# Wide matmuls over both activation halves, one pair (MLP: two panels) sooner in a two-block transformer kernel

## What is computed

```python
def swiglu(h, w_gate, w_up, w_down):
    return (jax.nn.silu(h @ w_gate) * (h @ w_up)) @ w_down
# block 1, per layer (D_FF = 2816), twice, with rmsnorm in front
x = x + 0.5 * swiglu(rmsnorm(x, norm_ffn1[layer]), ffn1_gate[layer], ffn1_up[layer], ffn1_down[layer])
# block 2 (D_FF_2 = 4096)
v2 = rmsnorm_2(h, g_pre_mlp[i])
f = jnp.square(jax.nn.relu(v2 @ w_up[i])) @ w_down[i]
```

## Time and profile before

| what | value |
| --- | --- |
| median of 3 runs | 1740.2 us (1740.07 to 1741.12) |
| the profiled execution: its time | 1740.54 us |
| its span in the trace | 1738.7 us |
| TensorE busy | 1711.1 us, 98% of the span |
| VectorE busy | 1129.2 us, 65% |
| ScalarE busy | 963.3 us, 55% |
| GpSimd busy | 139.7 us, 8% |
| HBM traffic | 166 GB/s over the span |
| granted TensorE clock, mean | 0.998 of full |

### The profile page before, as it was taken

One profiled execution on the slowest core, in us unless ns is written; L12 is line 12 of the kernel. 1 busy time (PEld: TensorE's weight loads), 2 busy tenths in 40 slices (PEclk: granted clock), 3 DMA queues, 4 the chain that ended last, 5 costly groups with the idle time before them and its releaser, 6 DMA issues.

```text
span 1738.7 us, 29426 instructions
## 1 busy us (share of the span) xinstructions
PE 1711.1 (98%) x12582; PEld 1537.9 (88%) x12582; DVE 1129.2 (65%) x1315; ACT 963.3 (55%) x1127; POOL 139.7 (8%) x124
## 2 busy tenths in 40 slices
PE   9999999999999999999999999999999999999996
PEld 8888999898889888999898889987898889988896
DVE  6666789575567556689675556664455566775657
ACT  5544696564446444587564446644445564654445
POOL 1000004000000000004100000693000000000000
PEclk9999999999999999999999999999999999999999
DMA  8565552255655665554146665564455425455550
GB/s 285 171 201 188 157 175 94 86 180 173 202 186 169 194 194 194 158 170 146 52 146 195 193 194 191 170 199 160 157 181 172 168 75 170 169 181 188 190 184 33
DMA packets 202897, 290.75 MB, mean 167 GB/s; under 512 B 4656, under 2 KB 162480, under 8 KB 202640
## 3 DMA queue, kind: packets, MB, share of 16 engines
q1 hardware_dynamic: 202320, 287.11, 51.1%
q0 software_dynamic: 448, 1.77, 0.3%
HBM read 287.81 MB, written 1.05 MB: 166 GB/s over the span
## 4 chain that ended last, share of the span: by engine, by line
PE 87%; DVE 6%; ACT 6%; issue 2%; DVEq 0%; ACTq 0%
PE colb L1024 56%; PE acc L1024 29%; ACT w_hi L1672 2%; DVE u L2312 2%; DVE w_lo L2210 1%; PE acc L1224 1%; PE colb L1590 0%; DVE x L2350 0%; DVE u L2349 0%; DVE arena L2497 0%; ACT rstd L1805 0%; ACT u_both L1919 0%; ACT op_hi L1824 0%; ACT rstd L1806 0%; PE colb L1445 0%
## 5 line engine op out<-in xcount | busy, mean ns | idle before, releaser
L2210 DVE TENSOR_TENSOR w_lo<-raw,w_hi 128x2048 fp32r<-128x2048 f32 x269 | 625.9, 2327 | 354.1 <-ACT w_hi L1672 353.4
L1672 ACT ACTIVATE w_hi<-raw 128x2048 fp32r<-128x2048 f32 x269 | 512.1, 1904 | 245.0 <-PE acc L1024 183.7
L1024 PE MATMUL colb<-u_both,w_hi 128*128 128x256 f32 (+1 forms) x2880 | 516.9, 334 | 0.6
L1024 PEld LDWEIGHTS colb<-u_both,w_hi 128*128 128x128 f32 x2880 | 438.8, 190 | 56.0 <-ACT u_both L1919 2.8
L1024 PE MATMUL colb<-u_both,w_lo 128*128 128x256 f32 x2112 | 274.7, 283 | 0.7 <-DVE w_lo L2210 0.7
L1024 PEld LDWEIGHTS colb<-u_both,w_lo 128*128 128x128 f32 x2112 | 267.9, 191 | 7.9 <-DVE w_lo L2210 1.4
L1024 PE MATMUL colb<-w_hi,u_both 128*128 128x512 f32 (+1 forms) x608 | 141.3, 381 | 0.0
L1024 PEld LDWEIGHTS colb<-w_hi,u_both 128*128 128x128 f32 x608 | 108.9, 188 | 21.1 <-issue 0.3
L1024 PE MATMUL acc<-op_hi,w_hi 128*128 128x256 f32 x544 | 97.1, 286 | 0.9 <-ACT arena L2070 0.9
L1024 PE MATMUL acc<-w_hi,op_hi 128*128 128x512 f32 x384 | 96.2, 392 | 0.0
L1024 PE MATMUL acc<-op_hi,w_lo 128*128 128x256 f32 x544 | 95.6, 284 | 0.2
(11 more groups left out here) (352 smaller groups left out, 1895.0 us busy)
## 6 DMA issues: line engine op xcount, KB each, us to landing
raw<-w_in SPq DMA_DIRECT2D x78, 1024.0 KB, 5.1
raw<-ffn_up SPq DMA_DIRECT2D x44, 1024.0 KB, 5.3
raw<-ffn_down SPq DMA_DIRECT2D x44, 1024.0 KB, 4.8
raw<-ffn_gate SPq DMA_DIRECT2D x43, 1024.0 KB, 5.3
raw<-w_up SPq DMA_DIRECT2D x16, 1024.0 KB, 5.5
raw<-w_down SPq DMA_DIRECT2D x16, 1024.0 KB, 4.9
raw<-w_out SPq DMA_DIRECT2D x8, 1024.0 KB, 4.9
raw<-w_ret_out SPq DMA_DIRECT2D x8, 1024.0 KB, 4.9
```

The costliest lines, as they stand in the source:

```text
L1024: return pe.matmul(o, a, b, start=start, stop=stop, skip_group_check=True)
L1672: act.activation(split_view(w_hi, r), raw[:, p % RAW_SLOTS, 0:r["kt"] * r["nc"]], ACT.Copy)\
L2210: tt(split_view(w_lo, r), raw[:, p % RAW_SLOTS, 0:r["kt"] * r["nc"]], split_view(w_hi, r).bitcast(F32), ALU.subtract).then_inc(sem("w_lo_r ...
```

## The change

The wide form begins at pair 1 instead of pair 2 in all feed-forwards but the very first (layer 0, `norm_ffn1`), and at panel 2 instead of panel 4 in the MLP. The MLP's operands 2 and 3 become ready by the vector engine's `relu2` instead of by ScalarE's ReLU and VectorE's square. Nothing else is touched.

```diff
             first_both = None
+            start_both = 2 if (layer, gain) == (0, "norm_ffn1") else 1
             for i in range(n):
                 g = panel(kpn(gate)[:, :, i * PC:(i + 1) * PC], KD, PC, "A", u_op, [("u_ready", 4 * f)],
                           by="act", evac=("silu_h", len(ops)))
-                if i == 2:
+                if i == start_both:
                     first_both = g["c"]
-                if i >= 2:
+                if i >= start_both:
                     two_banks(g, first_both, 0)
...
-                if i >= 2:
+                if i >= start_both:
                     two_banks(u, first_both, 1)
...
-            first_both = n_col + 4
+            first_both = n_col + 2
             for i in range(16):
                 up = kpn(ap["w_up_2"][0])[:, :, i * PC:(i + 1) * PC]
-                if i < 4:
+                if i < 2:
                     panel(up, KD, PC, "A", u_op, [("u_ready", 4 * f)], by="act", evac=("relu", len(ops)))
                     step("relu2", r=len(ops), evac=n_act)
...
-                r = operand(hid[:, len(ops) % 2, :], [("hid_ready", i + 1) if i < 4 else ("dve_evac", n_dve)]
+                r = operand(hid[:, len(ops) % 2, :], [("hid_ready", i + 1) if i < 2 else ("dve_evac", n_dve)]
```

## The result

The changed kernel takes 1764.95 us (median of 4 runs, 1763.58 to 1769.11) against 1740.66 (4 runs, 1740.07 to 1741.90). The ratio is 1.0137, with a 95% interval of 1.0126 to 1.0149: 24 us slower. The forecast of 1758.8 had the direction right, but the time lies 1.3 us above its range of 1753.4 to 1763.7.

The account below looks back on a forecast made before the run. The prediction took TensorE, busy 1711.1 of 1738.7 us, to bound the kernel. Waits at four places, less 0.4, gave 14.7 us, two clock falls 3.9, together 18.6, so a median of 1758.8 us, range 1753.4 to 1763.7.

Parts of the forecast that it names:

- the term for the clock: At the two idle stretches of 5.6 us, TensorE's clock falls to half: two times 1.95 us, 3.9 us in all.
- The waits: First down panels at the four places start 4.75, 4.75, 2.79 and 2.77 us later; less 0.4, 14.7 us.
- The copies, sums and splits: Extra ScalarE and VectorE passes behind the wide panels cost nothing, as the down panels' weight splits come in time.
- the whole 0.53: MLP's first down panel takes 0.53 us over the undisturbed one, its low split being late; 0.4 was given back.
- The clock, how often: The clock falls twice, at the 5.6 us stretches, and not at those of 3.6 and 3.9 us.
- The case with four falls: Rival: the clock falls at the shorter stretches too; 1762.7 us with four falls; three or four together have chance 0.15.
- The rule I cited beside that rival: Idle gaps between bursts of matmuls take the clock back to half; by it all four places would fall.
- The clock, its price: A fall means half rate for about 3.9 us, as at the run's start: 1.95 us lost each.
- The upper bound of 1.95 a place: The clock's price at each of the four places lies between nothing and 1.95 us, 7.8 in all.
- The banks don't bind: Rival: only the last low chunk holds the wide panels at all four places; 1750.9 us, chance 0.05.
- splits late: Rival: the SiLU waiting for VectorE holds the high split, down panels wait 1 to 2 us each; 1762 to 1767, chance 0.06.
- no wait at all: Rival: low halves and gate 0's bank are ready when PE arrives, so the change is faster; 1736.5 us, chance 0.03.

Follow-up runs that it names:

- Experiment 1: The changed kernel with 14 or 22 small matmuls of ones filling the idle stretch ahead of the first wide panel at the four places: 1757.68 us, ratio 1.0088.
- second profile: The changed kernel, with nothing altered, run and profiled once more: one execution of 1765.76 us, span 1763.9.
- experiments 2 to 6: 2: kernel before plus a wait for the last low chunk, 1761.27 us; 5 and 6: the change at one place alone, 1749.20 and 1746.11 us.
- experiment 3: The changed kernel, but its first wide panel waits for the low halves chunk by chunk, not for the last one: 1759.50 us, ratio 1.0102.
- experiment 4: The changed kernel with other PSUM banks for pair 1, so gate 1 never takes gate 0's bank: 1759.81 us, ratio 1.0099.
- experiment 6: The change at one place alone, the second feed-forward of layer 1, against the kernel before: 1746.11 us, ratio 1.0027.

## Why the prediction was wrong

The step that failed is the term for the clock: the prediction put it at 3.9 us, two falls of 1.95, and the two profiles of the change show 9.3 and 8.3, four falls of 2.2 on the mean. The rest of its sum held.

**The waits: right.** The forecast said 14.7 us. Experiment 1, which has them without a clock fall, is 14.5 us over before in span and 15.4 in the median. The bank bound at two places, the last low chunk at the other two, and each start and each step came within 0.4 us of the forecast.

**The copies, sums and splits: right.** No cost of them shows. In the MLP the first down panel takes 1567.03 - 1561.67 = 5.36 us, so the whole 0.53 came back where I had given 0.4. (The 2.5 ns a matmul that the prediction takes from the Trainium skill, page "TensorE: Matmul & The Clock Gate", section "Back-to-back issue gap", stand there for an isolated matmul, which it did not say; its sum goes by the 13 ns of the rows.)

**The clock, how often: wrong.** "I take it twice ... and not for the other two, which are hardly over it." It fell at all four. The case with four falls was a rival with 0.15, and it should have been the forecast: a single instance of a fall after 3.4 us was the only evidence, it spoke for a fall in stretches of 3.6 and 3.9 us (3.4 and 3.6 as measured), and nothing spoke against it. Nor is 3.4 us a mark to compare with: at the 20 waits counted below the clock fell 2.3 to 4.9 us after PE had stopped, at six of them when it was at work again. The rule I cited beside that rival, of the Trainium skill, page "TensorE: Matmul & The Clock Gate", said so too, and the traces agree: of 20 unbroken waits of 3.4 to 5.6 us in after, in its second profile and in experiments 2 to 6, all 20 had the clock fall; the two of 1.65 and 1.88 us in experiment 3 did not. A shorter wait is not safe either, though the prediction took it so ("the clock stays, as in all waits up to 1.9 us"): behind the 1.9 us wait near the run's end it fell in 6 of 14 profiles.

**The clock, its price: too small.** "Half the rate for about 3.9 us ... so 1.95 us lost", from the run's start. But a fall inside the run kept the clock low for longer: in layer 0 from about 375 to nearly 382, of which PE worked from 375.97 on, some 5.9 us. Half of that is 2.95; measured were 2.65. The eight falls of the two profiles cost 1.50 to 2.78 us, 2.2 on the mean, and they are of two kinds: in three the clock was low for 3.4 us and the price was 1.5, in five it was low for 6.8 us and the price was 2.4 to 2.8. The upper bound of 1.95 a place was no bound, since it was itself one instance. With 14.7 and the 9.3 of the profiled execution the sum is 1740.2 + 24.0 = 1764.2, with the 8.3 of the second 1763.2, and the median is 1764.95. Four falls at the prediction's own price would have given its 1762.7. So the count of the falls moved the forecast by 3.9 us, and their price by another 0.5 to 1.5; the price alone does not surely carry the time over the range's end of 1763.7.

The Trainium skill, same page, section "HAM oscillation — how this bites in real kernels", reckons the loss as the time at the low clock times (1 - 1.2/2.4). The layer 0 rows agree within about a tenth (2.95 reckoned, 2.65 measured), if only the low time with work in it is counted.

**What stands beside it.** Comparing the start of each matmul with that of the same one in before, the four places cost 7.6, 7.3, 5.7 and 3.9 us in the profiled execution, 24.4 together, and 7.7, 7.4, 4.4 and 3.9 in the second profile, 23.3. Less the 14.7 of waits that is 9.7 and 8.6, near the 9.3 and 8.3 counted at the marks. Of the 28.6 us of the first profile 2.5 more are the fall in the mixer and PE's pauses around it, 1.4 the fall at the run's end, and 0.3 scatter. The second profile has 0.6 in the mixer and 1.6 at the end. Its 1765.76 us are close to the median, so the median may well hold a fall at the end too, and whether that one belongs to the change is open.

**The rivals.** "The banks don't bind", "splits late" and "no wait at all" are refuted by the same rows. What I had called wrong signs (no idle stretch, stretches of one length, a time under 1750) did not appear; that the falls cost more than 2 us each was not on my list.

## What to carry to other kernels

A form that needs all of an operand before its first instruction trades many small waits for one long one on the engine that bounds the kernel. Price the wait from the readiness of the last chunk and from the bank, and then look at how long TensorE stands idle: count a clock fall for each stretch like those here (3.4 to 5.6 us), at 1.5 to 2.8 us. Before such a conversion, find work that needs only what is ready (here the low-weight matmuls), and ask what the wide form gives if all waits vanish: here it was 0.42 us a pair, less than the waits that remained.

## What the runs showed of the hardware that I had not expected

- A fall's price varied from 1.50 to 2.78 us, at one place (layer 1, second feed-forward) from 1.50 to 2.73 between two executions of the same kernel. The clock was low there from 924.4 to 927.8 in one and from 924.6 to 931.4 in the other. At the 20 waits it was low for 3.4 us ten times and for 6.8 us ten times.
- The fall need not come while PE is idle. In experiment 4 it came 1.5 us after PE had restarted in layer 0, behind a wait of 3.4 us (375.7, restart at 374.2).
- Four small matmuls in the midst of an idle stretch did not keep the clock: it fell 0.3 us behind their end in layer 0 (0.70 in the window 373 to 374). Fourteen or twenty-two, which filled the stretch, did keep it.
- The clock also falls in sparse stretches of work, in some executions and not in others: in the mixer of layer 1 with 2.17 us for 16 matmuls in one profile of after and 3.67 in the other, and behind a wait of only 1.9 us near the run's end in 6 of 14 profiles. Runs of one kernel lie up to 6.7 us apart (experiment 6, 1743.78 to 1750.48), so an effect of 1 us can't be read from one pair of spans, only from the differences between neighbouring marks in a trace.
